# Reordering the mixing stage of a two-layer encoder kernel, and running the first pair of experts ahead of its loop

## The reference, cut to what matters

```
h   = x @ w_in + b_in
c   = silu(LN(conv31(a * sigmoid(g))))                 # 256 channels, causal depthwise, 31 taps
att = softmax([q k^T / 8, sink]) v                     # 8 query heads, 2 kv heads, rotary on 16 dims, window of 128
gm  = u * (masked 128x128 mixing of LN(v))             # 256 channels
x   = LN(ALPHA * x + [c, att, gm] @ w_out + b_out)     # ALPHA = 4 ** 0.25
f   = sum over 16 experts of gate * (silu(x Wg) * (x Wu)) Wd    # two experts per token
x   = LN(ALPHA * x + f)
```

## Time and profile before

| what | value |
|---|---|
| median of 3 runs | 1068.28 us (1068.08 to 1070.03) |
| profiled execution, its own time | 1068.19 us |
| its span, first to last instruction | 1066.3 us |
| PE busy | 985.3 us, 92% |
| DVE busy | 809.4 us, 76% |
| ACT busy | 655.1 us, 61% |
| POOL busy | 539.8 us, 51% |
| mean granted clock of PE | 0.962 of full speed |

### The profile page before, as it was taken

One profiled execution on the slowest core, in us unless ns is written; L12 is line 12 of the kernel. 1 busy time (PEld: TensorE's weight loads), 2 busy tenths in 40 slices (PEclk: granted clock), 3 DMA queues, 4 the chain that ended last, 5 costly groups with the idle time before them and its releaser, 6 DMA issues.

```text
span 1066.3 us, 15510 instructions
## 1 busy us (share of the span) xinstructions
PE 985.3 (92%) x4852; PEld 792.6 (74%) x4852; DVE 809.4 (76%) x967; ACT 655.1 (61%) x737; POOL 539.8 (51%) x291
## 2 busy tenths in 40 slices
PE   7989998599999999999999979995999999999995
PEld 5876777488888888877778757774788888888882
DVE  5996757777878787777878977476877777777876
ACT  5324823377888787777533346323788787887861
POOL 1635354246566665545425354540656565656553
PEclk9998999599999999999999999996899999999998
DMA  9634293399999999995813211733999999999962
GB/s 291 222 89 174 69 335 125 134 318 354 359 346 367 342 333 342 354 344 174 251 53 119 79 49 40 291 143 116 324 372 362 360 365 360 356 362 333 368 218 82
DMA packets 122304, 268.51 MB, mean 252 GB/s; under 512 B 10523, under 2 KB 26043, under 8 KB 121760
## 3 DMA queue, kind: packets, MB, share of 16 engines
q1 hardware_dynamic: 111136, 247.14, 64.3%
q0 software_dynamic: 11136, 20.96, 7.4%
HBM read 259.19 MB, written 27.79 MB: 269 GB/s over the span
## 4 chain that ended last, share of the span: by engine, by line
PE 69%; DVE 21%; issue 3%; POOL 2%; ACT 2%; DVEq 1%; DMA 0%; SPq 0%; ACTq 0%
PE bank L776 34%; PE bank L794 17%; PE bank L431 9%; DVE bank L1173 7%; PE bank L754 2%; DVE xTl L1142 2%; POOL xtok L1621 1%; PE bank L748 1%; DVE moemem L1429 1%; DVE w_gate L1149 1%; PE bank L577 1%; DVE small L1194 1%; PE bank L829 1%; PE bank L825 1%; PE bank L544 1%
## 5 line engine op out<-in xcount | busy, mean ns | idle before, releaser
L1675 POOL TENSOR_TENSOR wl<-w_down,wh 128x2048 fp32r<-128x2048 f32 x33 | 151.8, 4601 | 148.8 <-ACT wh L1041 148.8
L1142 DVE TENSOR_TENSOR wl<-w_gate,wh 128x2048 fp32r<-128x2048 f32 (+1 forms) x75 | 169.5, 2260 | 53.1 <-ACT wh L1041 35.9
L1142 DVE TENSOR_TENSOR wl<-w_up,wh 128x2048 fp32r<-128x2048 f32 x66 | 151.2, 2293 | 29.2 <-ACT wh L1041 28.4
L1041 ACT ACTIVATE wh<-w_up 128x2048 fp32r<-128x2048 f32 x66 | 126.6, 1918 | 31.7 <-PE bank L794 21.7
L1041 ACT ACTIVATE wh<-w_down 128x2048 fp32r<-128x2048 f32 x66 | 126.7, 1920 | 31.0 <-PE bank L776 29.0
L776 PE MATMUL bank<-wl,xTh 128*128 128x512 f32 x528 | 144.0, 395 | 1.6 <-DVE wl L1142 1.6
L776 PE MATMUL bank<-wh,xTl 128*128 128x512 f32 x528 | 144.0, 395 | 1.1 <-DVE xTl L1142 1.1
L776 PE MATMUL bank<-wh,xTh 128*128 128x512 f32 x528 | 144.5, 396 | 0.2 <-ACT wh L1041 0.2
L1607 POOL TENSOR_TENSOR wl<-w_gate,wh 128x2048 fp32r<-128x2048 f32 x16 | 73.6, 4606 | 123.1 <-ACT wh L893 122.8
L1041 ACT ACTIVATE wh<-w_gate 128x2048 fp32r<-128x2048 f32 x66 | 126.5, 1916 | 12.8 <-PE bank L794 8.8
L1142 DVE TENSOR_TENSOR xTl<-bank,xTh 128x512 fp32r<-128x512 f32 (+1 forms) x168 | 89.8, 574 | 44.9 <-issue 21.4
(11 more groups left out here) (228 smaller groups left out, 1796.7 us busy)
## 6 DMA issues: line engine op xcount, KB each, us to landing
w_up<-in_exp_w_up SPq DMA_DIRECT2D x32, 2048.0 KB, 18.4
w_down<-in_exp_w_down SPq DMA_DIRECT2D x32, 2048.0 KB, 17.7
w_gate<-in_exp_w_gate SPq DMA_DIRECT2D x32, 2048.0 KB, 17.6
w_gate<-in_w_in SPq DMA_DIRECT2D x13, 1024.0 KB, 5.6
w_gate<-in_w_out SPq DMA_DIRECT2D x8, 1024.0 KB, 5.0
y_rows<-moemem SPq DMA_DIRECT2D x8, 512.0 KB, 9.4
x_rows<-xtok POOLq DMA_DIRECT2D x8, 512.0 KB, 3.0
w_up<-y_rows SPq DMA_DIRECT2D x8, 512.0 KB, 4.7
```

What stands on the lines that cost most here:

```text
L1041: act.activation(wh[s][:, :], slot[r][p][:, cols], ACT.Copy).then_inc(half_high, 1)
L1142: return dve.tensor_tensor(out, src, high.bitcast(F32), ALU.subtract)
L1675: pool.tensor_tensor(wl[s][:, :], slot[r][p][:, cols], wh[s][:, :].bitcast(F32), ALU.subtract)\
```

## The change

- PE: three blocks of the projection move forward by one place each: `channels(5, 1)` ahead of `conv_mean`, `channels(6, 0)` ahead of `scores(l, 1)`, `channels(6, 1)` ahead of `conv_spread`.
- DVE: the fifth rotation (k) and the masks move ahead of taps 20 to 25 of the second half; taps 20 to 30 run behind them without a break.
- POOL: the low part of piece 7 waits for `mask_set`, that of piece 8 for the second `pn_done` of the layer. The four multiplications of `xtok` by ALPHA go; `b_out` is divided by ALPHA instead, once, and DVE's `add_mix` multiplies by ALPHA while it adds the product.
- ACT, DVE and POOL: `chunk_loops` takes the first pair of experts out of the loop and loads three chunk starts first. On DVE `late_out`, and on POOL the waits for `tab_set` and `late_set`, come behind these loads.

```diff
-        def chunk_loops(eng, l, body):
-            with eng.Fori(0, E // 2) as pair:
+        def chunk_loops(eng, l, body, ready=None):
+            starts = [first_chunk(eng, l, e) for e in range(3)]
+            if ready:
+                ready()
+            for r in range(2):
+                with eng.Fori(starts[r], starts[r + 1]) as c:
+                    body(c, 0, r)
+            with eng.Fori(1, E // 2) as pair:
                 starts = [first_chunk(eng, l, 2 * pair + r) for r in range(2)]
...
                 scores(l, 0)
+                channels(5, 1)
                 conv_mean(l)
-                channels(5, 1)
+                channels(6, 0)
                 scores(l, 1)
                 turn_probs(l, 0)
                 turn_gates(l)
                 conv_var(l)
-                channels(6, 0)
+                channels(6, 1)
                 conv_spread(l)
                 scores(l, 2)
-                channels(6, 1)
...
-                link(dve.tensor_tensor(x, x, bank[4 * n + j][:, :], ALU.add))
+                link(dve.scalar_tensor_tensor(x, x, ALPHA, bank[4 * n + j][:, :], ALU.mult, ALU.add))
...
-                for n, hi in enumerate((8, 14, 20, 26)):
+                for n, hi in enumerate((8, 14, 20)):
                     rope(l, n, qr[:, n, :])
                     taps(1, hi - (4 if n == 0 else 6), hi)
+                rope(l, 3, qr[:, 3, :])
                 rope(l, 4, kr)
...
-                taps(1, 26, TAPS)
+                taps(1, 20, TAPS)
...
-                late_out(l)
-                chunk_loops(dve, l, lambda c, pair, r: chunk(l, c, pair, r))
+                dve.wait_ge(start_set, l + 1)
+                chunk_loops(dve, l, lambda c, pair, r: chunk(l, c, pair, r), lambda: late_out(l))
...
+                pool.wait_ge(mask_set, l + 1)
                 piece_lows(l, 7)
...
-                if l == 0:
-                    pool.wait_ge(xtok_in, 16)
-                else:
-                    pool.wait_ge(tr_done, TT * 2 * l)
-                for j in range(TT):
-                    link(pool.tensor_scalar(xtok[:, j, :], xtok[:, j, :], ALPHA, None, ALU.mult))
...
+                pool.wait_ge(pn_done, TT * l + 2)
                 piece_lows(l, 8)
                 piece_lows(l, 9)

                 pool.wait_ge(rows_in, 32 * l + 16)
+                link(pool.tensor_scalar(rows3[:, 0, :], rows3[:, 0, :], 1.0 / ALPHA, None, ALU.mult))
+                if l == 0:
+                    pool.wait_ge(xtok_in, 16)
+                else:
+                    pool.wait_ge(tr_done, TT * 2 * l)
                 for j in range(TT):
                     pool.tensor_tensor(xtok[:, j, :], xtok[:, j, :], rows3[:, 0, :], ALU.add).then_inc(xb_done, 1)
...
-                pool.wait_ge(tab_set, l + 1)
-                pool.wait_ge(late_set, l + 1)
-                chunk_loops(pool, l, lambda c, pair, r: chunk(l, c, r))
+                def tables():
+                    pool.wait_ge(tab_set, l + 1)
+                    pool.wait_ge(late_set, l + 1)
+                chunk_loops(pool, l, lambda c, pair, r: chunk(l, c, r), tables)
```

## The result

The changed kernel takes 1053.36 us (median of 4 runs, 1050.89 to 1053.66), the kernel before 1068.18 (1067.48 to 1070.03) beside it: a ratio of 0.9855, 95% interval 0.984 to 0.987. It is 14.8 us faster. The forecast had the sign and half of the size, and its range began 1.6 us too high. The profiled execution took 1053.41 us by itself, with a span of 1051.6.

A forecast was written before the change was run, and what follows sets the result against it. PE was taken to bound the kernel (69% of the chain of waits, DVE 21%), losing time idle or at half clock. 1068.2 - 8.4 (mixing) + 4.0 (clock) - 3.0 (experts' start) = 1060.8 us, range 1055 to 1068.

The forecast's parts named there:

- The rotation before the taps and the mask at 73: Mixing, before the first scores: mask comes at about 73, `conv_mean` ends 2.0 us sooner, 1.6 in layer 1.
- L1206 begins 5.5 us sooner: DVE's third softmax: with L1194 no longer locked by POOL, L1206 ends at 111.9, not 117.85, 6.0 us sooner.
- `conv_lows` is locked for 1.5 us: DVE behind L1206: `conv_lows` waits 1.6 us for POOL's piece 8, leaving `turn_probs(2)` 4.4 us sooner, 4.0 in layer 1.
- The loads of the chunk starts: Experts' start: loads move into DVE's idle 2.04 us, about 0.2 of loop entry stays; 1.5 us gained per layer.
- the clock holding in both layers: Rival for PE's quiet place before the second `turn_probs`: full clock stays, 1056.8 us; chance 0.20.
- The rival that the lock isn't POOL's: Third softmax: L1194's 4.2 us are not POOL's, gain 2.0 per layer less clock, 1065 us; chance 0.06.
- the loop start that gains nothing: Rival at the experts: entering the loop after the first pair costs another 1.80 us, 1063.8 us; chance 0.08.
- the price of the clock, -8.4 + 4.0: Mixing gains 8.4 us; a clock fall in PE's quiet place (full cost 5.5) was taken at 2.0 per layer, 4.0 lost.
- I keep the 7.17 us block as it is.: Mixing, PE's block of 24 multiplications before the third scores: stays at 7.17 us, though 5.5 at full clock.
- the experts' start, -3.0: Gates to the first chunk: 1.5 us sooner per layer, between 0.8 and 2.5 (the clock rises sooner too).
- ALPHA's removal: Beside DVE's first softmax: frees DVE but the projection block covers it; nothing counted, up to 2.9 us without the cover.
- At piece 10: DVE's low part beside POOL's `xtok` additions: between 0 and 1.1 us of PE waiting per layer, taken as 0.

The follow-up runs named there:

- pn_only: Kernel before with one edit: POOL's piece 8 waits for the second `pn_done`; 1064.06 us, ratio 0.9954.
- no_pn: Changed kernel without POOL's wait for the second `pn_done`; 1062.47 us, ratio 0.9949.
- loop_only: Kernel before with only the new `chunk_loops` (first pair outside the loop, chunk starts loaded early); 1063.77 us, ratio 0.9954.
- before: The kernel before, unchanged, in its first profile; median 1068.18 us.
- before_again: The kernel before, unchanged, run once more for a second profile; 1069.29 us, ratio 1.0007.
- after: The changed kernel with the whole change, in its first profile; 1053.36 us, ratio 0.9855.
- after_again: The changed kernel run once more for a second profile; 1053.42 us, ratio 0.9858.
- mixing_only: Changed kernel with the old `chunk_loops` of the kernel before; 1056.88 us, ratio 0.9891.
- loads_late: Changed kernel with the three chunk starts loaded after the gates and table waits, first pair still outside the loop; 1060.41 us, ratio 0.9925.
- busy_routing: Changed kernel plus 28 and 12 unused PE multiplications in two waits of the routing; 1052.32 us, ratio 0.9857.
- busy_all: Changed kernel plus unused PE multiplications: 11 before `turn_probs(1)`, 28 and 12 in the routing, 4 before `conv_var`; 1049.39 us, ratio 0.9822.
- before_busy: Kernel before plus 28 and 12 unused PE multiplications during the routing; 1067.35 us, ratio 0.999.
- order_only: Kernel before with PE's and DVE's new orders; POOL, ALPHA and the loop left as they were; 1077.55 us, ratio 1.0076.
- no_mask: Changed kernel without POOL's wait for the mask (`mask_set`); 1063.73 us, ratio 0.996.
- alpha_back: Changed kernel with POOL's four ALPHA multiplications returned and `add_mix` a plain addition; 1056.55 us, ratio 0.9888.

## Why the prediction was wrong in size

**Right, with its number.** The rotation before the taps and the mask at 73: `conv_mean` ends 1.94 us sooner after `turn_values` in layer 0 (forecast 2.0) and 1.62 in layer 1 (1.6). Piece 7 beside taps costs nothing (0.66 us each). L1206 begins 5.5 us sooner, 6.3 against `turn_values` (6.0), and `conv_lows` is locked for 1.5 us (1.6). The loads of the chunk starts: 1.87 and 1.60 us in waits (1.5). The rival whose time came nearest, the clock holding in both layers (1056.8), is not what happened: the clock fell in both. The rival that the lock isn't POOL's is out by `pn_only` and `no_pn`, and the loop start that gains nothing by `loop_only` (0.9954).

**Wrong: the price of the clock, -8.4 + 4.0.** The clock did fall in both layers, as the step had it; its size was wrong. I had all small pieces and half of `out_first(0)` at half clock. In the profile after it lasts from 112 to 119 us: `turn_probs(1)` costs 0.9 and the scores 2.15, the pieces behind them next to nothing, and 1.8 of the 3.0 lie in waits for ACT and DVE. Nor was it "near one fall in two": by the clock records it fell in all twelve layers, for 3.4 us in four of them, which cost nothing, and for 6.8 us in eight, which cost 0.3 to 1.2. Twelve layers give 0.5 instead of 2.0: 3.0 us of the 7.4 missed. (The full fall was also added up slightly wrong: 5.7 us of pieces grown by 1.8 make PE 2.8 us late, not 2.6; the 2.0 taken doesn't hang on it.)

**Wrong: the clock of `channels(6, 1)`.** "I keep the 7.17 us block as it is." In the changed kernel's layer 1 it took 5.58 (chain of waits of the changed kernel, where layer 0 still has 7.17):
```profile
98.01 7.17 PE bank L437 x24
...
629.76 5.58 PE bank L437 x24
```
Scores(1) to scores(2) took 15.4 us in all four layers of `before` and `before_again`. In the ten layers of `after`, `after_again`, `mixing_only`, `loads_late` and `busy_routing` it took 13.8 us four times, 15.4 five times and 17.0 once, in the mean 14.9: 0.5 per layer. Where the fall fails to come, DVE meets POOL's gate scaling (L1200 takes 0.97 us in layer 1 of the changed kernel), which gives 0.8 back, some 0.3 per layer in the mean. What decides whether the clock falls there stays open: `busy_all` rules out the short wait ahead of it alone. PE's old order (`before`, `before_again`, `before_busy`, `loop_only`, `pn_only`) has 15.4 in all ten layers, and the two kernels whose first scores came late and at half clock, `order_only` and `no_mask`, have 13.8 in all four; so it goes with what PE does earlier in the stage, but which part of that decides isn't shown.

**Wrong: the experts' start, -3.0.** The waits were right, and the clock's return was the mis-sized half. My bounds named it (up to 2.5), and I took nothing for it. Measured are 1.05 us per layer from low part to L754, where the clock's rise sets the time, beside 1.73 of waits: 2.8 against the 1.5 taken, 2.6 us of the 7.4 missed, and `loop_only` gives 2.45 per layer by its time. Since the same stretch of the kernel before scatters from 9.3 to 12.0, only the mean can be trusted.

**A term missed, one that came out even.** ALPHA's removal I counted at nothing because the block covers it. Had the multiplications stayed, 0.5 to 0.6 us per layer would have come through, as PE is there 2 us sooner; it is the cover for the 2.0 at `conv_mean`, not a gain beside it. The 0.3 per layer in the routing are a gain beside it, which I had no term for. At piece 10 DVE got in (2.34 us, not 4.27) and POOL's additions grew from 9.57 to 11.51 instead; nothing on PE waited. The multiplication of `b_out` took 2.79 us, as the rows of before had it (2.85), where the figure of the Trainium skill (GPSIMD Engine Reference, § 3.1) gave an estimate of 0.9.

Summed by the means: the mixing is 4.4 per layer (49.7 over the six layers with the old mixing in `before`, `before_again` and `loop_only`, 45.3 over the ten of the new). Its parts are 1.8 at `conv_mean`, 0.2 in the block behind it, 2.55 from the lock (scores(2) to `turn_probs(2)`, 16.25 to 13.70 where the clock holds), less 0.5 for the clock, 0.5 at `channels(6, 1)` less 0.3 given back: 4.25. With 2.8 at the start and 0.3 in the routing (the ALPHA edit's, see above) this is 7.5 per layer, 15.0 us, less 0.5 in the rest of the experts (1.0 lost in layer 0 as above; from L754 of layer 1 to the end 306.3 us against 306.75): 14.5 of the measured 14.8. The range was too narrow since its lower end added one piece of luck (1.8 us) to the case in which the clock holds, though the start's own bound alone reached 2.0.

## What to carry to other kernels

A wait that holds back an engine with a shared port can be worth more than the work it delays: the same new order of instructions was 0.76% slower without the two waits on POOL and, with the waits, the ALPHA edit and the loop, 1.45% faster. When a wait makes PE's clock fall, price only what exceeds the next wait for another engine, and ask in the same way whether a shorter wait brings the clock back sooner. A stretch measured between two named instructions, over a dozen layers of related kernels, settles sub-microsecond terms that medians of whole runs can't.

## What was not expected of the hardware

DVE and POOL share in both directions: in the changed kernel DVE's subtraction of piece 10 took 2.34 us while POOL's four additions grew to 11.51 us (9.57 before), and in `alpha_back` it took 4.23 beside additions of 9.55. Eight-column instructions on DVE (0.17 us) are held like large ones (4.25 in `order_only`). It also goes the other way for the smallest instruction: a one-column operation of POOL took 1.54 us instead of 0.56 when DVE's L1306 had started 0.17 us before it. Twelve multiplications between the routing's steps (`busy_routing`, until 193.1 us) did not keep the clock at its higher level through the sparse products behind them: it was at the lower level when the chunk's first four began (2.07 us).
